# One core, two transformer blocks: the mixer's output projection and the norms behind it by token halves

## The reference, cut to what matters

```python
def first_block(x, c, ada_w, ...):
    mod = jax.nn.silu(c) @ ada_w + ada_b              # 6 x 1024 numbers
    sh1, sc1, ga1, sh2, sc2, ga2 = split(mod, 6)
    h = rmsnorm(x, pre_mix_g) * (1.0 + sc1) + sh1
    y = hybrid_mixer(h, ...)                          # ends in: merged @ w_o
    x = x + ga1 * rmsnorm(y, post_mix_g)
    h = rmsnorm(x, pre_ffn_g) * (1.0 + sc2) + sh2
    y = swiglu_ffn(h, w_ffn_in, w_ffn_out)            # (silu(gate) * up) @ w_ffn_out
    x = x + ga2 * rmsnorm(y, post_ffn_g)
```

## Time and profile before

| | |
|---|---|
| time, median of 3 runs | 1393.56 us (1392.45 to 1394.81) |
| profiled execution, time | 1392.63 us |
| its span | 1390.8 us |
| granted TensorE clock, mean | 0.993 |
| TensorE matmul busy | 1342.9 us (97%) |
| VectorE busy | 992.1 us (71%) |
| ScalarE busy | 700.2 us (50%) |
| GpSimd busy | 101.5 us (7%) |

### The profile page before, as it was taken

The page is one execution under the profiler, slowest core; times in us unless marked ns, Lnnn a source line. Parts: engine busy times, 40 slices in busy tenths (PEclk is TensorE's granted clock), DMA queues, the critical chain, the costliest instruction groups (busy, mean ns, idle before and its releaser), DMA issues. The chain is left out here.

```text
span 1390.8 us, 18712 instructions
## 1 busy us (share of the span) xinstructions
PE 1342.9 (97%) x7213; PEld 1148.7 (83%) x7213; DVE 992.1 (71%) x1229; ACT 700.2 (50%) x957; POOL 101.5 (7%) x73
## 2 busy tenths in 40 slices
PE   7999999999889999999999999989999999999997
PEld 5789788877668989988999897778878888888886
DVE  4899988778878679846848758888557745663663
ACT  4323777683445535533545755669355423441434
POOL 0000000011100194000012000000110000000002
PEclk9999999999999999999999999999999999999999
DMA  9444211046532343232251161220323232322222
GB/s 376 186 170 111 86 60 45 30 152 242 226 121 104 117 181 123 91 122 89 86 190 69 61 167 46 59 55 1 116 74 113 91 103 85 115 90 91 91 68 83
DMA packets 28871, 156.14 MB, mean 112 GB/s; under 512 B 3264, under 2 KB 5824, under 8 KB 15616
## 3 DMA queue, kind: packets, MB, share of 16 engines
q1 hardware_dynamic: 28800, 155.17, 31.5%
HBM read 145.98 MB, written 4.19 MB: 108 GB/s over the span
## 5 line engine op out<-in xcount | busy, mean ns | idle before, releaser
L1846 DVE TENSOR_TENSOR w_lo<-raw,w_hi 128x2048 fp32r<-128x2048 f32 (+3 forms) x135 | 252.3, 1869 | 83.5 <-ACT w_hi L1121 70.2
L1121 ACT ACTIVATE w_hi<-raw 128x2048 fp32r<-128x2048 f32 (+2 forms) x84 | 150.3, 1789 | 103.6 <-PE psum L616 62.7
L616 PE MATMUL psum<-h_hi,w_hi 128*128 128x512 f32 x376 | 96.2, 394 | 1.5 <-DVE w_lo L1846 1.3
L616 PE MATMUL psum<-h_hi,w_lo 128*128 128x512 f32 x376 | 95.1, 391 | 0.0
L616 PE MATMUL psum<-h_lo,w_hi 128*128 128x512 f32 x376 | 94.3, 389 | 0.0
L616 PEld LDWEIGHTS psum<-h_hi,w_hi 128*128 128x128 f32 x376 | 69.0, 188 | 17.0 <-DVE w_lo L1846 3.2
L616 PE MATMUL psum<-xg_lo,w_hi 128*128 128x512 f32 x336 | 83.0, 389 | 0.0
L616 PE MATMUL psum<-xg_hi,w_lo 128*128 128x512 f32 x336 | 83.0, 389 | 0.0
L616 PE MATMUL psum<-xg_hi,w_hi 128*128 128x512 f32 x336 | 83.0, 389 | 0.0
L616 PEld LDWEIGHTS psum<-h_lo,w_hi 128*128 128x128 f32 x376 | 70.6, 188 | 14.7
L616 PEld LDWEIGHTS psum<-h_hi,w_lo 128*128 128x128 f32 x376 | 70.0, 188 | 14.5
(11 more groups left out here) (433 smaller groups left out, 3085.5 us busy)
## 6 DMA issues: line engine op xcount, KB each, us to landing
raw<-w_ffn_in SPq DMA_DIRECT2D x22, 1024.0 KB, 4.8
raw<-w_up SPq DMA_DIRECT2D x22, 1024.0 KB, 4.8
ada_first<-ada SPq DMA_DIRECT2D x16, 512.0 KB, 11.5
raw<-w_gate SPq DMA_DIRECT2D x8, 1024.0 KB, 4.9
raw<-w_mix_out SPq DMA_DIRECT2D x8, 1024.0 KB, 5.4
raw<-w_ffn_out SPq DMA_DIRECT2D x8, 1024.0 KB, 4.9
raw<-w_down SPq DMA_DIRECT2D x8, 1024.0 KB, 4.8
ada_mid<-ada SPq DMA_DIRECT2D x11, 512.0 KB, 5.2
```

Source lines behind the costliest of these rows:

```text
L616: last = mm(ps, w[slot][:, k, t * P:(t + 1) * P], part(xv, k0 + k), start=first, stop=final)
L1121: A(w_hi[slot][:, 0:stage.kc, :], raw[slot][:, 0:stage.kc, :], ACT.Copy).then_inc(sem["w_hi_done"], 1)
L1846: return tt(out_lo, full, high.bitcast(F32), ALU.subtract)
```

## The change

`mix_out` keeps all four weight groups on the chip (`mix_hi`, `mix_lo`) and runs them for tokens 0-255, then for tokens 256-511. Both norms of the seam go by halves (`post_mix_a`, `pre_ffn_a`, `post_mix_b`, `pre_ffn_b`), and so do groups 0 and 1 of `ffn_in0`: both for the first half, then both for the second. The modulation's 18 columns come in batches of 5, 7, 5 and 1 in other buffers; five of them move into `att_out`, and one batch of seven tiles is loaded ahead of `conv_out`'s groups 2 and 3. The load of the table of ln and exp moves to the start of `mix_out`. Rows with `...` are cut.

```diff
-ADA_MIX = [5, 6, 7]
+ADA_MIX = [5, 7, 5, 1]
...
-    mix_bufs = [[ada_side[0]] + ada_x, ada_mid, ada_side + ada_mid[0:5]]
+    mix_bufs = [ada_x[1:] + [ada_side[0], ada_x[0]], ada_x + [ada_side[0]] + ada_h[2:4],
+                [ada_side[1]] + ada_h[0:2] + ada_h[4:6], [ada_side[0]]]
...  SyncE
+            sp.wait_ge(sem["ada_sum"], ADA_AT[0])
+            load_tiles(mix_bufs[0][:4], ADA_AT[0], "ada_tiles")
             stage_loads(st["gate"], 1)
             stage_loads(st["att_out"])
             sp.wait_ge(sem["o_evac"], HEADS)
-            load_tiles(mix_bufs[0], ADA_AT[0], "ada_tiles")
-            stage_loads(st["conv_out"])
+            load_tiles(mix_bufs[0][4:], ADA_AT[0] + 4, "ada_tiles")
+            for k in range(2):
+                load(st["conv_out"], k, k)
+            sp.wait_ge(sem["ada_sum"], ADA_AT[1])
+            sp.wait_ge(sem["tile_done"], 2 * st["conv_out"].g0)
+            load_tiles(mix_bufs[1], ADA_AT[1], "ada_tiles")
+            for k in range(2, 4):
+                load(st["conv_out"], k, k - 2)
             for k in range(2):
                 load(st["mix_out"], k, k)
-            sp.wait_ge(sem["mid_f"], DC)
-            load_tiles(mix_bufs[1], ADA_AT[1], "ada_tiles")
+            sp.wait_ge(sem["tile_done"], 2 * st["mix_out"].g0)
+            load_tiles(mix_bufs[2], ADA_AT[2], "ada_tiles")
             load(st["mix_out"], 2, 0)
-            sp.wait_ge(sem["ada_sum"], ADA_AT[1])
+            sp.wait_ge(sem["ada_sum"], ADA_AT[1] + 5)
             sp.dma_start(x[:, :, :], dram["x"]).then_inc(sem["in_rows"], 16)
-            load_tiles(mix_bufs[2][0:2], ADA_AT[2], "ada_tiles")
             load(st["mix_out"], 3, 1)
-            sp.wait_ge(sem["ada_sum"], ADA_AT[2])
-            load_tiles(mix_bufs[2][2:], ADA_AT[2] + 2, "ada_tiles")
+            sp.wait_ge(sem["ada_tiles"], ada_tiles(3))
+            load_tiles(mix_bufs[3], ADA_AT[3], "ada_tiles")
...  TensorE
-            gemm(st["mix_out"], mid_hi, mid_lo, ready=("mid_lo_done", 0, 0))
-            stat_sum_and_last("post_mix")
-            stat_chunks("pre_ffn")
+            for k in range(4):
+                pe.wait_ge(sem["w_lo_done"], mo.g0 + k + 1)
...              # side_group for k == 0, else two side_tile calls, tokens 0-255
+            for k in range(4):
+                for t in range(2):
+                    if (k, t) == (0, 1):
+                        stat_sum_and_last("post_mix_a", SIDES[0], bank[0])
+                    elif (k, t) == (3, 0):
+                        mix_stat(0)
+                    side_tile(side_of(4 + k, t), SIDE_SLOT[SIDE_ORDER[1][k]], t, DC, mid_hi, mid_lo, SIDES[1], ...)
+            for a in range(2):
+                pe.wait_ge(sem["w_lo_done"], fi.g0 + 1)
+                if a:
+                    pe.wait_ge(sem["ms_done"], rstds("pre_ffn_b") + 1)
+                side_group(..., h_hi, h_lo, SIDES[a], ("made_lo", MADE["pre_ffn"] + DC * a),
+                           beside=None if a else lambda: stat_sum_and_last("post_mix_b", SIDES[1], bank[4]))
+                pe.wait_ge(sem["w_lo_done"], fi.g0 + 2)
...              # two side_tile calls, then for a == 0:
+                    mix_stat(1)
...  side_group, used by the second seam too
-                    if beside and k == 2:
+                    if beside and k == 3:
...  ScalarE
+            nc.scalar.preload_act_table_set("natural_log_exp_and_others")
+            for k in range(4):
+                if k < 3:
+                    mix_split(k + 1)
+                mix_evac(0, k)
...              # post_mix_a, mix_evac(1, 0), next_split(0), new_squares(0), mix_evac(1, 1), next_split(1),
...              # pre_ffn_a, first_high(0) with mix_evac(1, 2) and (1, 3) between, post_mix_b, new_squares(1),
...              # pre_ffn_b, first_high(1)
...  VectorE, in att_out: columns 0-2 of the batch of five at k == 0, 3 and 4 at k == 2; then
+            mix_low(1)
+            columns(1, 0, 4, ada_tiles(2))
+            mix_low(2)
+            columns(1, 4, 7, ada_tiles(2))
+            mix_low(3)
+            columns(2, 0, 3, ada_tiles(3))
+            dve.wait_ge(sem["rs_done"], 3)
+            dve.wait_ge(sem["in_rows"], 16)
+            mix_update(0)
+            columns(2, 3, 5, ada_tiles(3))
+            columns(3, 0, 1, ada_tiles(4))
...
+            mix_sum(0)
+            split_lo(fi, 0, 0)
+            dve.wait_ge(sem["rs_done"], 4)
+            first_made(0)
+            split_lo(fi, 1, 1)
+            dve.wait_ge(sem["rs_done"], 5)
+            mix_update(1)
+            mix_sum(1)
+            dve.wait_ge(sem["rs_done"], 6)
+            first_made(1)
...  beside ffn_in0's whole groups, in the evacuation of group k, both engines
-                    if k + 1 < FOLDS["ffn_in0"]:
-                        split_lo(first, k + 1, (k + 1) % 2)
-                    else:
+                    if k < 2:
+                        split_lo(first, k + 2, k)
+                    elif k == 3:
                         fold_split(first, k + 1)
```

More of the change, by code:

```diff
@@ new lines, in side_group @@
+            def side_group(into, one_bank, kc, x_hi, x_lo, cols, ready, beside=None):
+                for k in range(kc):
+                    if beside and k == 3:
+                        beside()
+                    pe.wait_ge(sem[ready[0]], ready[1] + k + 1)
+                    for t in range(2):
+                        for n, (w, xv) in enumerate(((w_hi, x_hi), (w_lo, x_hi), (w_hi, x_lo))):
+                            last = mm(into[t], w[0][:, k, t * P:(t + 1) * P], xv[:, k, cols],
+                                      start=(n == 0 and k == 0 and not (one_bank and t)), stop=(n == 2 and k == kc - 1),
+                                      skip_group_check=True)
+                        if cols is not SIDES[0] and k == kc - 1:
+                            last.then_inc(sem["tile_done"], 1)
+                return last
@@ new lines, in side_of, with mix_stat @@
+            def side_of(b, t):
+                return bank[b][:, t * (S // 2):(t + 1) * (S // 2)]
+            mo, fi = st["mix_out"], st["ffn_in0"]
+            def mix_stat(a):
+                pe.wait_ge(sem["sum_x"], 2 * a + 2)
+                o_ps_read(("pre_ffn_a", "pre_ffn_b")[a])
+                into = bank[(1, 4)[a]][:, SIDES[a]]
+                mm(into, ones[:, :], sq_x[a][:, 0, :], start=True, stop=False)
+                mm(into, ones[:, :], sq_x[a][:, 1, :], start=False, stop=True).then_inc(sem["stat_done"], 1)
@@ L1408, in _ @@
             run(st["conv_out"], merged)
-            run(st["mix_out"], to_y(st["mix_out"], "post_mix"))
-            norm_rstd("post_mix", D)
-            squares("pre_ffn", lambda c: x[:, c, :], lambda c: act.wait_ge(sem["x_new"], c + 1))
-            norm_rstd("pre_ffn", D, load=False)
-            act.wait_ge(sem["ada_sum"], ADA_AT[3])
-            for c in range(DC):
-                made(MADE["pre_ffn"] + c, h_hi[:, c, :], mod[:, 3 * DC + c:3 * DC + c + 1])
+            nc.scalar.preload_act_table_set("natural_log_exp_and_others")
@@ new lines, in _ @@
+            act.wait_ge(sem["gain_done"], 1)
+            for k in range(4):
+                if k < 3:
+                    mix_split(k + 1)
+                mix_evac(0, k)
+            norm_rstd("post_mix_a", D, load=False, src=bank[0], cols=SIDES[0])
+            mix_evac(1, 0)
+            next_split(0)
+            for part in range(2):
+                new_squares(0, part)
+            mix_evac(1, 1)
+            next_split(1)
+            norm_rstd("pre_ffn_a", D, load=False, src=bank[1], cols=SIDES[0])
@@ L1418, in gated @@
+            act.wait_ge(sem["ada_sum"], ADA_AT[4])
+            first_high(0, range(2))
+            mix_evac(1, 2)
+            first_high(0, range(2, 5))
+            mix_evac(1, 3)
+            first_high(0, range(5, DC))
+            norm_rstd("post_mix_b", D, load=False, src=bank[4], cols=SIDES[1])
+            for part in range(2):
+                new_squares(1, part)
+            norm_rstd("pre_ffn_b", D, load=False, src=bank[4], cols=SIDES[1])
+            first_high(1, range(DC))
             def gated(stage):
@@ L2107, in convolved, with columns @@
                 return u[:, c, PAD:PAD + S] if c < 2 else sums[c - 2][:, :]
+            def columns(batch, begin, end, landed):
+                dve.wait_ge(sem["ada_tiles"], landed)
+                for r in range(begin, end):
+                    ada_column(mix_bufs[batch][r], ADA_AT[batch] + r)
             def gate_att(i, s, k, ahead):
@@ L2185, in add_normed @@
[L2185 to L2190 removed]
+                        dve.wait_ge(sem["made_hi"], m0 + c)
+                        if a == 0 and b == DC // 2:
+                            dve.wait_ge(sem["tile_done"], 2 * mo.g0 + 6)
+                        stt(h_lo[:, b, cols], t_n[b % 2][:, cols], mod[:, 3 * DC + b:3 * DC + b + 1], h_hi[:, b, cols].bitcast(F32),
+                            ALU.add, ALU.subtract).then_inc(sem["made_lo"], 1)
```

208 lines of the change are left out of this document (132 added, 76 removed).

## The result

| | kernel before | kernel after |
|---|---|---|
| median of the runs | 1394.18 us | 1415.98 us |
| ratio, 95% interval | | 1.016 [1.0148, 1.0173] |
| profiled execution, span | 1392.63, 1390.8 us | 1415.2, 1413.4 us |
| mean granted clock | 0.993 | 0.987 |

The direction was right and the size was not: the profiled execution lost 22.6 us where the prediction summed 11.7, and the time lies above its range of 1398 to 1411.

What follows compares the result with a forecast made beforehand. TensorE, busy for 97% of the span, was taken as the bound. Terms 2.0 + 2.5 + 8.6 - 1.4 = 11.7 us onto 1392.63 gave 1404.3, as a median 1405.3; range of 8 in 10, 1398 to 1411.

Steps and rivals of the forecast that it cites:

- the main loss: `mix_out`'s first half: group 3, loaded behind `x`, makes TensorE wait 11.1 us, with 2.6 us of slow clock after.
- r: Time in us counted from the start of `mix_out` on TensorE.
- The wait before group 1: `mix_out`'s first half: TensorE waits 3.0 us for group 1, whose split stands behind the table load of 1.28 us.
- X: End of group 3 in `mix_out`'s first half on TensorE, predicted at 41.1 us after `mix_out` starts.
- the first chain: First half's norm, up to its chunks for `ffn_in0` from about X + 21.5: hidden behind the second half's matmuls, by 3 us.
- the second half's two waits: Before `ffn_in0`'s second half, the second norm is not hidden: TensorE waits 1.4 and, after two matmuls, 2.6 us.
- parts 1 and 2: Three columns in `att_out`, 2.0 us, and seven tiles ahead of `conv_out`'s group 2, 2.5 us: `mix_out` starts 4.5 us late.
- one fall of the clock: Slow clock counted once in the sum: 2.6 us behind the wait of 11.1 us in `mix_out`'s first half.
- its highest end of 1413 us: All terms at their highest, with 2.9 and once more 2.6 us of slow clock and no gains: +19.7 us.
- the gain at group 3: `ffn_in0`: the wait of 0.69 us before group 3 goes, as its split comes earlier; part of 1.4 us of gains.
- The prediction's other gain: Second seam: `beside` one chunk later covers the wait of 0.63 us; part of 1.4 us of gains.
- X to group 2: From the end of `mix_out`'s first half to the start of group 2 of `ffn_in0`: 57.4 us.

Runs made afterwards that it cites:

- e3: Kernel after with `conv_out`'s weight group 2 loaded ahead of the seven tiles; 1411.89 us, 1.0126 against the kernel before.
- e1: Kernel after with the load of `mix_out`'s group 3 moved ahead of the load of `x`; 1403.46 us, 1.0076 against the kernel before.
- e10: e9 plus 6 and 9 added matmuls of constants on TensorE in the second norm's two waits; 1392.3 us, 0.9995 against the kernel before.
- e2: Kernel after with the three columns in `att_out` moved behind the gates of group 1; 1409.92 us, 1.0117 against the kernel before.
- e6: Kernel after with 36 unused matmuls of constants in the wait before `mix_out`'s group 3; 1413.03 us, 1.0141 against the kernel before.
- e7: Kernel after with the edits of e1, e2 and e3 together; 1398.22 us, 1.0035 against the kernel before.
- e8: e7 with ScalarE's high halves of the folded inputs moved behind the Silu of group 1; 1394.45 us, 1.0008 against the kernel before.
- e4: Kernel after with block sums and high halves of the folded inputs behind the gating of groups 0 and 1; 1412.55 us, 1.0135 against before.
- e9: e8 with the table load and ScalarE's split of `mix_out`'s group 1 moved earlier, into idle time; 1392.44 us, 0.999 against the kernel before.

## Why the prediction was right, and where it fell short

**Right: the mechanism of the main loss.** `x` ahead of group 3 was priced at a wait of 11.1 and 2.6 us of slow clock; the profile after has 9.66 and 5.26 us for 24 matmuls against 2.87 at full rate (24 x 0.1195), 2.4. ScalarE waited 10.08 us for the DMA and its high half started at 362.46, r = 27.9, against 28.5. The wait before group 1 was 2.85 against 3.0. X came 0.8 us earlier than worked out: 0.6 as the weights landed sooner and 0.2 in the slow clock. Group 2 had no wait of its own where 1.3 us were expected, which changes nothing, as the long wait behind it ends when the weights are there.

```profile
345.04 1.91 ACT L1474 ACTIVATE w_hi<-raw 128x2048 fp32r<-128x2048 f32 x1 [2.71 <-DMA raw<-w_mix_out]
...
362.46 1.91 ACT L1474 ACTIVATE mix_hi<-raw 128x2048 fp32r<-128x2048 f32 x1 [10.08 <-DMA raw<-w_mix_out]
```

**Right: the first chain is hidden.** `ffn_in0` starts at 400.06, X + 25.2 (predicted X + 24.8), without a wait, and the second half's two waits are 1.69 and 2.68 (1.4 and 2.6).

**Right in kind, low in size: parts 1 and 2.** They came to 7.6 us instead of 4.5: `conv_out` starts 3.6 us later (305.93 against 302.31, 2.0 expected), and takes 4.0 us longer (28.64 against 24.68, 2.5 expected). The collisions were all three full ones, VectorE's and GpSimd's timelines of the kernel after:

```profile
283.91 2.30 DVE L2086 CUSTOM_DVE_ANT_0 ada_x<-ada_x,c_row,vec 128x1024 f32<-128x1024 f32 x1
...
286.15 2.30 DVE L2086 CUSTOM_DVE_ANT_0 ada_x<-ada_x,c_row,vec 128x1024 f32<-128x1024 f32 x1
...
288.38 2.30 DVE L2086 CUSTOM_DVE_ANT_0 ada_x<-ada_x,c_row,vec 128x1024 f32<-128x1024 f32 x1
```

```profile
283.60 6.01 POOL L2939 TENSOR_TENSOR sq_sum<-sq_sum,sq 128x512 f32<-128x512 f32 x3
```

VectorE resumes its gates at 290.72, 2.65 us later than in the earlier trace rows; the prediction's own highest value for this, 2.5, was the right one, and its reason for 2.0, that the two engines run side by side, speaks for 2.5. GpSimd's three additions grew from 4.41 to 6.01 us too. That is what the Trainium skill says ("SBUF — State Buffer", "Who interferes with whom"), and the trace agrees with all three. The transfer was nearly sized right: from SyncE's issue of the tiles at 306.08 to ScalarE's split at 318.75 are 12.7 us, where 12.4 were worked out. So of the 3.1 us missing here 0.65 are the collision, 0.3 the transfer, and 2.1 the clock, the next point.

**The step that failed, the first: one fall of the clock.** The sum has 2.6 us of slow clock once, for the wait of 11.1 us, and gives the waits of 2 to 3 us none; a second fall stood only in its highest end of 1413 us, which the range then left out. (Added up again from their terms, its two ends are +3.7 and +19.5 us and not +3.9 and +19.7, which changes nothing.) The windows behind six waits of the kernel after:

```profile
293.20:296.70 3.50, 3.50 (x9) 2.73 (x10) 2.27 (x3) 3.44 (x4) 0.00 (x0) 0.54 0.53 157
321.12:324.10 2.98, 2.98 (x7) 2.41 (x8) 2.91 (x5) 0.98 (x2) 0.00 (x0) 0.50 0.71 201
343.43:346.40 2.97, 2.97 (x18) 2.97 (x19) 2.97 (x5) 1.36 (x1) 1.73 (x2) 0.71 0.26 105
418.53:422.70 4.17, 4.17 (x19) 4.17 (x20) 4.03 (x10) 2.12 (x5) 0.00 (x0) 0.50 0.67 273
435.05:438.00 2.95, 2.95 (x13) 2.48 (x14) 1.29 (x2) 2.32 (x2) 0.00 (x0) 1.00 0.42 172
449.83:453.20 3.37, 3.37 (x9) 2.65 (x10) 2.82 (x3) 1.00 (x2) 0.00 (x0) 0.60 0.00 0
```

Five of the six are slow. Against the full rate (0.227 us for a matmul of 512 columns, 0.1195 for one of 256) they lose 3.50 - 9 x 0.227 = 1.5, 1.4, 0.8, 1.9 and 1.3 us, 6.9 together, and the prediction's 2.6 stands for the seventh. Not all of it reaches the end, as a comparison with the traces in which the same stretch ran at the full clock shows:
- The first costs 1.6: from the third group of `att_out` to `conv_out` are 12.73 us here and 11.12 and 11.15 in e3 and e1.
- The second costs 1.4 - 0.9 = 0.5, as the wait at `mix_out`'s start fell from 1.73 to 0.86 us.
- The third vanishes in the wait of 9.66 us.
- The fourth costs 0.9: from the first chunk of the second half to group 2 are 16.52 us here and 15.60 in e10. VectorE's pace hides the rest.
- The last costs nothing. From the start of group 2 to the second folded product are 30.4 us in the kernel after (435.05 to 465.47) and in e1, e2, e3, e6 and e7, whichever of the groups ran slow. In e1 group 3 ran at 1.00, and TensorE then waited 1.60 us at that product:

```profile
437.82:441.20 3.38, 3.38 (x15) 2.79 (x16) 2.83 (x3) 1.00 (x2) 0.00 (x0) 1.00 0.00 0
```

```profile
453.46 0.75 PE L863 MATMUL psum<-t_hi,fold_hi 128*128 128x256 f32 x4 [1.60 <-ACT psum L1204]
```

So 1.6 + 0.5 + 0.9 = 3.0 us of the missing 10.9 are clock, an estimate from one trace of each kernel. The trace had shown the price once, at a wait of 3.99 us, and I took shorter waits as safe without a row that said so. The Trainium skill's sentence on oscillation ("TensorE: Matmul & The Clock Gate") spoke of a kernel that falls again and again; I cited it and counted it once.

**The step that failed, the second: the gain at group 3.** The prediction had the wait of 0.69 us before group 3 of `ffn_in0` go, "as its split comes earlier". It became 3.66 us: the stretch from group 2 to the first folded group is 4.6 us longer, and 4.3 to the second folded product (30.4 against 26.1), where 0.7 less was predicted. I had looked at the queue of VectorE, block sums ahead of the gating, for group 2, and found 2.6 us there (2.73 measured). For group 3 I looked at the split only. But ScalarE's high halves stand ahead of the group's Silu in its own program and wait for VectorE's last block sum. Before, the sums began at 404.90, 12.0 us ahead of group 2; now they begin at 430.81, 4.2 us ahead of it, as the chunks of the second half are made right before. VectorE's timeline of the kernel after:

```profile
430.81 3.49 DVE L2445 TENSOR_TENSOR t_f<-h_hi,h_lo 128x1024 f32<-128x1024 f32 x3
...
449.00 0.69 DVE L2377 TENSOR_TENSOR act_p<-act_a,psum 128x512 f32<-128x512 f32 x1 [3.50 <-ACT act_a L1543]
```

e8 shows this cause alone: 3.8 us by the medians on top of e7, and 3.2 of these 4.3 us in the trace. The last 1.1 us stay in e8 too, with its wait of 1.93 us for ScalarE at the second folded product (0.29 before). This term is the largest that the sum missed. The prediction's other gain, the 0.63 us in the second seam, was a small one: 0.38 us of that wait stay.

**In size only: X to group 2** took 60.2 us for 57.4. The second half's group 0 began at X + 43.65 (predicted 42.2), and groups 0 and 1 took 16.5 - 2.7 = 13.8 us for 12.6, 0.9 of it the clock.

What stays open is why the clock fell behind one short wait and not behind another, and what makes ScalarE late for the last 1.1 us. The spread of e3 and e4, 1407 to 1414 and 1409 to 1414 us, would fit a clock that falls in some executions only, as near 149 us in e3; only one execution of each has a trace.

## What to carry to other kernels

When a stage is cut in halves its weights are needed twice as fast, and whatever large load stands in front of the next group in the queue is now the bound: write each group's load ahead of loads that are needed later, before anything else is tuned (12 us for two lines exchanged here). Price each new wait with the slow clock behind it, also the short ones, and then ask what stands behind: a later wait can cover the slow clock as it can cover another wait, and then neither is added. For each instruction that frees a bank, read both engines' programs ahead of it: what waits there for a third engine delays the bank though nobody is busy.

## What the hardware showed

- The same wait at the same place is followed by either clock level. Behind 2.41 us before `att_out`'s third group the kernel after ran at 0.54, and e3 behind 2.42 us at 1.00; behind 2.85 us before `mix_out`'s group 1 the figures are 0.71 and 1.00. 2.51 us in e4 brought 0.50, 2.73 us before group 2 of `ffn_in0` 1.00. The third group cost 1.6 us more where the clock fell. The windows of e3:

```profile
341.46:345.00 3.54, 3.54 (x29) 3.54 (x30) 3.54 (x5) 1.92 (x1) 1.73 (x2) 1.00 0.02 5
...
296.79:300.00 3.21, 3.21 (x14) 2.67 (x15) 2.36 (x4) 3.18 (x3) 0.00 (x0) 1.00 0.48 163
```

- A column on VectorE beside GpSimd's additions takes 2.30 us instead of 1.28, and the three additions 6.0 instead of 4.4: both engines lose, and the first three columns each lost the same.
- Seven tiles and a group, 4096 KB, were ready for ScalarE 12.7 us after the first issue in the kernel after, 12.5 in e2 (304.40 to 316.86) and in e6, against the 12.4 of the earlier trace rows. But e1 and e4, with the same batch, took 13.8 (303.52 to 317.37 in e1). So the time of a batch could be worked out from two rows to within 0.3 us in three traces of five, and was 1.4 us short in two; why is open.
- The profiled executions of these kernels reached the seam at times up to 4.8 us apart, though they are the same program up to there (VectorE's `u<-u,mean` at 280.09 in e1, 284.67 in e3, 284.86 in e9). Stretches between two points of the seam agree far better: 30.4 us in six kernels. Times of single executions should be compared by stretches.
